# Prompt's attention in a decoder step: probabilities turned two units behind their scores, products with the values three units behind

## What is computed

```
x <- LN1(alpha*x + 0.5*SwiGLU_1(x))
x <- LN2(alpha*x + W_o [ DSA_heads(x) | MLA_heads(x) ])
x <- LN3(alpha*x + 0.5*SwiGLU_2(x))
```

```
s = (einsum('bqhr,bkr->bhqk', ql, c_kv) + einsum('bqhd,bkd->bhqk', qp, k_pe)) * scale      # MLA
p = softmax(where(key_pos <= pos, s, -inf));  o = einsum('bhqk,bkr->bqhr', p, c_kv)
score = einsum('bqh,bqhk->bqk', wi, relu(einsum('bqhd,bkd->bqhk', qi, k_idx)))             # DSA
sel = top_k(score);  p = softmax(einsum('bqhd,bqkd->bqhk', qa, k[sel]) * AD**-0.5);  o = p v
```

## Time and profile before

| | |
|---|---|
| median of 3 runs | 3186.89 us (3186.84 to 3187.45) |
| profiled execution | 3187.09 us, its span 3185.4 us |
| TensorE matmuls busy in the span | 2956.1 us (93%) |
| VectorE, ScalarE, GpSimd busy | 1414.1 (44%), 1003.1 (31%), 641.8 us (20%) |
| first layer's prompt block | about 645 to 842 us, busy: TensorE 167.4, VectorE 154.4, ScalarE 90.2 us |
| second layer's | about 2212 to 2412 us, busy: 169.6, 155.1, 91.4 us |

### The profile page before, as it was taken

One profiled execution on the slowest core, in us unless ns is written; L12 is line 12 of the kernel. 1 busy time (PEld: TensorE's weight loads), 2 busy tenths in 40 slices (PEclk: granted clock), 3 DMA queues, 4 the chain that ended last, 5 costly groups with the idle time before them and its releaser, 6 DMA issues. The chain is left out here.

```text
span 3185.4 us, 45574 instructions
## 1 busy us (share of the span) xinstructions
PE 2956.1 (93%) x18282; PEld 2540.3 (80%) x18298; DVE 1414.1 (44%) x2116; ACT 1003.1 (31%) x1614; POOL 641.8 (20%) x562
## 2 busy tenths in 40 slices
PE   7999999888898889999999999997888988999997
PEld 7999879655576689998799997785656666999975
DVE  2222364468764452222632223734887445322236
ACT  2222243454443332222322222335444433222223
POOL 1111021231123141110221110412302133211103
PEclk9999999899999999999999999998999999999998
DMA  4222452400123322224422224413001234222243
GB/s 117 80 81 83 133 157 72 142 1 1 67 85 129 101 85 79 79 81 137 158 87 79 79 89 142 148 51 133 1 17 67 85 113 144 68 79 79 92 144 124
DMA packets 241737, 293.79 MB, mean 92 GB/s; under 512 B 12624, under 2 KB 205488, under 8 KB 235456
## 3 DMA queue, kind: packets, MB, share of 16 engines
q1 hardware_dynamic: 234688, 229.00, 23.5%
q0 software_dynamic: 6912, 62.92, 5.4%
HBM read 287.72 MB, written 3.88 MB: 92 GB/s over the span
## 5 line engine op out<-in xcount | busy, mean ns | idle before, releaser
L159 DVE TENSOR_TENSOR wlo<-raw,whi 128x1024 fp32r<-128x1024 f32 (+2 forms) x398 | 514.8, 1294 | 1295.0 <-ACT whi L153 1294.0
L153 ACT ACTIVATE whi<-raw 128x1024 fp32r<-128x1024 f32 (+2 forms) x398 | 418.5, 1053 | 1435.6 <-PE ps L608 864.6
L608 PE MATMUL ps<-xth,whi 128*128 128x296 f32 x2624 | 752.0, 299 | 5.4 <-PEq L770 5.4
L608 PE MATMUL ps<-xtl,whi 128*128 128x296 f32 x2624 | 754.6, 300 | 0.0
L608 PE MATMUL ps<-xth,wlo 128*128 128x296 f32 x2624 | 571.7, 300 | 0.0
L608 PEld LDWEIGHTS ps<-xth,whi 128*128 128x128 f32 x2624 | 494.6, 188 | 5.5 <-issue 5.5
L608 PEld LDWEIGHTS ps<-xtl,whi 128*128 128x128 f32 x2624 | 493.3, 188 | 0.0
L608 PEld LDWEIGHTS ps<-xth,wlo 128*128 128x128 f32 x2624 | 427.5, 188 | 0.0
L166 PE MATMUL ps<-whi,hth 128*128 128x512 f32 (+1 forms) x880 | 350.6, 398 | 9.9 <-DVE wlo L159 8.3
L168 PE MATMUL ps<-whi,htl 128*128 128x512 f32 (+1 forms) x880 | 346.9, 394 | 0.0
L167 PE MATMUL ps<-wlo,hth 128*128 128x512 f32 (+1 forms) x880 | 346.7, 394 | 0.0
(11 more groups left out here) (404 smaller groups left out, 4380.6 us busy)
## 6 DMA issues: line engine op xcount, KB each, us to landing
raw<-in_ffn_w_in SPq DMA_DIRECT2D x176, 512.0 KB, 3.8
raw<-in_ffn_w_out SPq DMA_DIRECT2D x176, 512.0 KB, 3.5
raw<-in_w_o SPq DMA_DIRECT2D x32, 512.0 KB, 3.4
raw<-in_w_in SPq DMA_DIRECT2D x16, 507.0 KB, 3.9
gb<-in_ln_g SPq DMA_DIRECT2D x6, 512.0 KB, 5.6
gb<-in_ln_b SPq DMA_DIRECT2D x6, 512.0 KB, 6.3
raw<-in_w_in SPq DMA_DIRECT2D x8, 338.0 KB, 3.9
x<-in_x_prompt SPq DMA_DIRECT2D x1, 1536.0 KB, 10.6
```

Of the source, the lines that this page charges most:

```text
L153: e.activation(dst, T.raw[:, s, 0:width], ACT.Copy).then_inc(S.hi_done, 1)
L159: e.tensor_tensor(w_lo, T.raw[:, s, 0:width], w_hi.bitcast(F32), ALU.subtract).then_inc(S.split_done, 1)
L608: mm = e.matmul(bank(u, up)[:, h, :], part[:, s, w], xp[:, k, o], start=(k == 0 and part is T.whi and xp is T.xth), stop=(k == KD - 1 and ...
```

## The change

Every stage from the transposes on goes one step later: transposes i-2, product i-3, and ScalarE's copy i-2, in step i; the division of a group is three steps behind its last unit, the transposes of `posb` four, the `uv` product five. The plan has one step more. The number of buffers and all instructions stay.

```diff
-    lag = n + 6
+    lag = n + 7
...
-        if 0 <= i - 1 < n:
-            for part in range(2 if units[i - 1][1] == 4 else 1):
+        if 0 <= i - 2 < n:
+            for part in range(2 if units[i - 2][1] == 4 else 1):
...
-        if 0 <= i - 2 < n:
-            p["pv"] = i - 2
-        if i - 2 in last:
-            p["norm"] = last[i - 2]
-        if i - 4 in last and last[i - 4][0] == "M":
-            p["uv"] = (b_job, last[i - 4][1])
+        if 0 <= i - 3 < n:
+            p["pv"] = i - 3
+        if i - 3 in last:
+            p["norm"] = last[i - 3]
+        if i - 5 in last and last[i - 5][0] == "M":
+            p["uv"] = (b_job, last[i - 5][1])
...
-        if i - 3 in last:
-            kind, t = last[i - 3]
+        if i - 4 in last:
+            kind, t = last[i - 4]
...
-    tjob = {i - 1: p["t"][-1] for i, p in enumerate(plan) if p["t"]}
+    tjob = {i - 2: p["t"][-1] for i, p in enumerate(plan) if p["t"]}
...
-                    u = i - 1
+                    u = i - 2
...
-                    e.wait_ge(S.pv_done, i - 1)
+                    e.wait_ge(S.pv_done, i - 2)
```

## The result

The changed kernel takes 3203.21 us (median of 5 runs, 3199.81 to 3206.43), the kernel before 3187.45 us (5 runs, 3186.84 to 3188.02): ratio 1.0049 [1.0035, 1.0064], 15.8 us slower. That is slower by more than 0.2%, and outside my range. The profiled execution took 3205.84 us, its span is 3204.1 us against 3185.4. One execution of `a_warm` took 11371 us and is left out of that run's ratio.

The account below looks back on a forecast made before the run. It took VectorE to set the pace in M2, elsewhere a loop of VectorE and TensorE or hand-overs. Per layer -0.4 + 1.0 - 0.5 + 0.5 = +0.6, two layers +1.2, giving 3188.1 us; range 3183 to 3194.

Parts of the forecast that it names:

- The copy: In every unit, the wait before the transposes only moves to the product, which waits for ScalarE's copy; 0 gained.
- Rival 1: At five places a layer the transposes' time, 0.44 us each, is won; 3183.7 us, chance 0.12.
- rival 2: All VectorE waits outside the index units are freed, 8.5 us a layer; 3169.8 us, chance 0.03.
- The head: Pipeline filling at M0's start: one pass of transposes and products leaves it; -0.4 us a layer (-0.8 to 0).
- The drain: After D4's last scores TensorE has four blocks left instead of two; +1.0 us a layer (0 to +1.6).
- D3: Hand-over M3 to D3: VectorE's stall falls from 3.27 to about 3.27-1.24 us; net -0.5 a layer (-2.0 to 0).
- M1: Hand-over D0 to M1: equal rounds, or a stall that only moves; 0.
- D1, M2, D2, the step that failed: Hand-overs into these groups: the chain behind posb keeps its length; +0.5, 0 and 0 us a layer.
- D0: Hand-over M0 to D0: equal rounds, or a stall that only moves; 0.
- M3: Hand-over D2 to M3: one round behind posb instead of two, a new stall replaces two; 0 (-1.5 to +1.4 us).
- rival 3: Less VectorE work behind posb at M2, M3; D2's h2 uncovered: up to 4.6 us a layer slower, 3196 us, chance 0.09.
- rival 4: Changed posb waits give two TensorE clock falls less or more a layer, 0.98 us each; 3184.2 or 3192.0, chance 0.16.

Follow-up runs that it names:

- a_warm: Experiment 1: the changed kernel with one to four useless matmuls on TensorE while it waits for posb at six groups; 3187.18 us, 0.9997 of the kernel before.
- experiment 9: The changed kernel with ScalarE's copy i-2 put ahead of exponential i in each step; 3200.36 us, 1.0035 of the kernel before.
- b_warm: Experiment 2: the kernel before with one or two useless matmuls in TensorE's waits for posb at D0, D1, M2, M3, D3; 3182.03 us, ratio 0.9981.
- experiment 6: The changed kernel with the last tile's two extra jobs one unit later, before D2's h3 and h5; 3199.96 us, 1.0041 of the kernel before.
- experiment 3: The changed kernel run once more with nothing altered; 3203.84 us, 1.0046 of the kernel before.
- experiment 5: The kernel before with one round moved ahead of posb in M2 and M3, plus useless matmuls in the waits for posb; 3184.57 us, ratio 0.9991.

## Why the prediction was wrong

- **The copy** (0 a unit, 22.1 us of waits only moved): right. The stretches that hold nothing else agree within 0.02 us, the waits reappear before the products, and experiment 9 shows them to be slack, but for 0.3 us a layer ahead of D4.
- **Rival 1** (the transposes' time won) and **rival 2** (8.5 us a layer freed): wrong, as judged.
- **The head** (-0.4): -0.6 and -0.2 with D0's start. The rows behind it lie where the clock was 0.50 (656 to 660 us), which I didn't see. **The drain** (+1.0): +1.3. D4's transposes (848.43) are 1.59 us behind its exponential's end (846.84), as predicted; the rest of the chain is 0.3 longer than I took.
- **D3** (-0.5): right in place and a little small, -0.6 and -1.4. The stall stands before h4, at 1.86 us, where h3 had 3.27; I had taken 3.27 - 1.24 = 2.03. That the sum came near is partly luck: with the clock kept in both kernels D3 wins only 0.3 us (14.63 and 14.32), the rest is that it fell less there. **M1**, which I took for 0, gained 0.55: its product waited 0.90 us for `posb` and now doesn't wait.
- **D1, M2, D2, the step that failed.** "This chain keeps its length; what VectorE does meanwhile is now unit h3's work instead of h2's, and h2's rounds now stand ahead of posb." The second half was right and should have ended the first. TensorE gets to its wait earlier by the waits that it no longer has, and `posb` comes later by h2's rounds: the waits for `posb` went from 1.00 to 2.46 us at D1, 2.20 to 3.58 at M2, 0.53 to 1.56 at D2. Behind them the chain didn't keep its length, because its matmuls took nearly twice as long (at M2 0.91 and 1.62 us, 0.81 and 1.49), at D2 in one layer only. I had +0.5, 0 and 0; it was +1.9, +2.4 and +3.0 (1.3 in the second layer). D1's +0.5 is about what the order alone costs (0.7 and 0.5, experiments 1 and 2); the clock is what the term had at nothing.
- **D0**, another 0 of mine, is the same step: +0.8 and +1.1. I counted it among the equal rounds, but its table has none in h2 and two in h3, and h2's samples' step now stands ahead of `posb`; the wait went from 1.84 to 2.45 us. **M3** (0) was +0.8 and -0.9, its clock having fallen in both kernels.
- **D2's two jobs.** I listed only the first (as the fourth tile's index job), in rival 3, as what holds h2's scores once `posb` no longer covers them. The sum job went inside the chain that I called unchanged. Together they cost 1.3 us a layer (13.92 against 12.59), by experiment 6.
- **The clock** was rival 4, at two falls of 0.98 us either way. The price counted only the eight products; a fall lasts over `posb`'s transposes and the next scores as well. With it kept, D0 is 2.4 us shorter, D1 1.2, M2 1.8, D2 1.6, M3 1.7, D3 1.35 (first layer, `a_warm` against the change), 10.1 together (7.3 in the second). The size hangs on the execution: in that of experiment 3 D2, M3 and D3 lost nothing in the first layer, and the same sum is 3.9 there. And the sign was not open: five of the six waits that are left became longer (only D3's fell, 2.36 to 2.08), and that leans to slower. I had the two rows in hand and didn't ask which further waits would become as long; and my line that the trace falls only behind these two missed D0 (0.67 behind 1.84 us) and the block's start.
- **Rival 3** was the right side: 3196 with 0.09. That 9.2 us comes nearer to the 15.8 than my sum is in part luck: the order and the drain together cost 5.1 us with the clock kept, less than it says, and the clock, which it left out, the rest. Its price of one round (1.4 us) is right for M3 in experiment 5 and wrong for M2 (0.08). I judged it by "a later stall goes there".

The Trainium skill (TensorE: Matmul & The Clock Gate, "What's actually happening") has the clock low by default and released by TensorE's own activity; experiments 1, 2 and 5 agree, with 1.00 at M2 in experiment 1, where idle products fill the wait, and 0.55 in the change, where they don't. Of the rule that I cited in the prediction, that small idle pieces throttle the array again and again, no stretch here shows anything: the copy's 21 waits (15.3 us) come and go with 0.3 us of change in the stretches that have no hand-over.

## What to carry over

In engines that work through their queues in order, a stage that is put one step later moves its waits to the next operand that isn't ready; ask first which that is. Then look at each hand-over: does TensorE now come earlier to one long wait, does the producer come later, and which jobs at fixed unit numbers now stand inside the chain behind it? Tables of fillers must be moved with the stages, and where a long wait remains and a chain behind it sets the pace, work of no use during the wait can be worth several us.

## What I had not expected of the hardware

- In the first layer six waits for `posb` of 1.6 to 3.6 us cost 10.1 us by the clock alone in one execution, and 3.9 in another. Their length alone doesn't say whether the clock falls: behind 2.20 us (M2 before) it stayed at 1.00, behind 2.36 us (D3 before) it was 0.50. Behind 3.31 us (M3 after) it fell in one execution and stayed at 1.00 in the other, and behind 1.56 us (D2 after) it was 0.66 in 770 to 775 us of the first layer and 1.00 in the second (2345 to 2350 us).
- The same program had its falls at different places in two executions (first block 189.0 and 183.0 us). The Trainium skill (TensorE: Matmul & The Clock Gate, "What's actually happening") has the gate watch activity in windows that run freely of the kernel; that fits falls that change their place, but no run here shows the windows themselves.
- Idle products cost under 0.1 us where they fit into the wait (M2 13.82 us with them in `b_warm`, 13.84 before), and brought 16 us in the changed kernel and 6 in the one before. Where they were one too many (M2 in `a_warm`), the products started 0.7 us later. Which number is best at each place was not searched for.
